# Score steps reordered over ticks, and three pieces of vector work spread, in a two-layer hybrid decoder kernel

## The reference

```
z    = x W_in                                   # 13 feature tiles, 4 value tiles, 10 gate tiles
o    = [GLA heads | retention heads | HGRN2 heads](z)      # gated linear recurrences
x    = LayerNorm(ALPHA x + o W_out)
q    = x W_q ; s1, s2 = q subkeys               # 8 heads, 2 x 128 keys
top 16 of s1, of s2, then of the 256 sums       # 16 experts a head, 128 a token
x    = LayerNorm(ALPHA x + sum_e gate_e gelu(u_e . x) v_e) # u_e, v_e: gathered rows of 1024
x    = x + (p W_ple) sigmoid(x W_gate)          # "embedding"
```

```
score[i, j] = sum_k q[i, k] k[j, k] exp(b[i, k] - b[j, k])   for j <= i,  b = running sum of log decay
```

## Time and profile before

| what | value |
|---|---|
| timed runs | 4085.25, 4070.53, 4074.74 us, median 4074.74 |
| profiled execution, own time | 4068.89 us |
| its span | 4067.1 us |
| granted TensorE clock, mean | 0.94 |
| busy: TensorE, VectorE, ScalarE, GpSimd | 3526.3, 2538.4, 1025.4, 2533.5 us |
| DMA read from HBM | 1259.74 MB, mean 312 GB/s with what was written |

### The profile page before, as it was taken

One profiled execution on the slowest core, in us unless ns is written; L12 is line 12 of the kernel. 1 busy time (PEld: TensorE's weight loads), 2 busy tenths in 40 slices (PEclk: granted clock), 3 DMA queues, 4 the chain that ended last, 5 costly groups with the idle time before them and its releaser, 6 DMA issues. The chain is left out here.

```text
span 4067.1 us, 42088 instructions
## 1 busy us (share of the span) xinstructions
PE 3526.3 (87%) x13480; PEld 2019.6 (50%) x13480; DVE 2538.4 (62%) x6604; ACT 1025.4 (25%) x2150; POOL 2533.5 (62%) x2420
## 2 busy tenths in 40 slices
PE   8787698999999799798999799999999877787878
PEld 6576364555555365344566256545555434222434
DVE  2535986766357985667557985567636798645442
ACT  2231132332122223222322222233312222211211
POOL 0212447877675655877765655687766666777773
PEclk9778799999999899999999999999999989999999
DMA  5015888888999898888999988888999989999996
GB/s 183 21 64 183 287 328 320 302 322 328 350 356 372 324 354 333 320 312 294 349 340 386 364 289 318 290 320 308 339 336 343 379 301 358 385 374 362 370 398 228
DMA packets 331050, 1270.02 MB, mean 312 GB/s; under 512 B 38336, under 2 KB 39616, under 8 KB 313808
## 3 DMA queue, kind: packets, MB, share of 16 engines
q0 software_dynamic: 299520, 1090.65, 73.0%
q1 hardware_dynamic: 31312, 176.67, 11.4%
HBM read 1259.74 MB, written 7.44 MB: 312 GB/s over the span
## 5 line engine op out<-in xcount | busy, mean ns | idle before, releaser
L819 PE MATMUL Y<-GV,DIAG 128*128 128x512 f32 x4096 | 1993.3, 624 | 315.4 <-DMA GV<-in_vtab,IDX 249.9
L1759 DVE SCALAR_TENSOR_TENSOR GU<-GU,X 128x1024 f32<-128x1024 f32 x1024 | 1241.4, 1230 | 511.2 <-DMA GU<-in_utab,IDX 508.9
L1038 POOL DMA_INDIRECT GU<-in_utab,IDX x1024 | 1152.5, 1125 | 641.4 <-DVE GU L1759 295.8
L1038 POOL DMA_INDIRECT GV<-in_vtab,IDX x1024 | 1146.1, 1119 | 597.8 <-PE Y L819 374.2
L819 PEld LDWEIGHTS Y<-GV,DIAG 128*128 128x128 f32 x4096 | 767.2, 197 | 1285.1 <-issue 985.9
L514 PE MATMUL A<-XT,WR 128*128 128x264 f32 (+1 forms) x2496 | 579.8, 388 | 18.1 <-ACT R L1252 10.5
L1285 ACT ACTIVATE DIAG<-C,WGT 128x128 f32<-128x128 f32 x1024 | 371.5, 392 | 749.1 <-PE Y L819 625.8
L514 PEld LDWEIGHTS A<-XT,WR 128*128 128x128 f32 x2496 | 481.3, 193 | 146.2 <-issue 74.9
L974 POOL TENSOR_TENSOR R<-R 128x256 f32<-128x256 f32 (+3 forms) x256 | 130.1, 541 | 164.6 <-DVE R L1437 88.9
L567 PE MATMUL SCP<-R,C 128*32 128x64 f32 (+3 forms) x512 | 104.6, 361 | 109.9 <-DVE R L1469 109.6
L733 PE MATMUL D<-WR,R 96*128 96x256 f32 (+3 forms) x800 | 189.9, 395 | 11.5 <-POOL R L992 11.5
(11 more groups left out here) (216 smaller groups left out, 2897.3 us busy)
## 6 DMA issues: line engine op xcount, KB each, us to landing
WR<-in_wstream SPq DMA_DIRECT2D x96, 1024.0 KB, 7.8
WR<-in_wstream SPq DMA_DIRECT2D x36, 1280.0 KB, 9.1
GU<-in_utab,IDX POOLq DMA_INDIRECT x1024, 6.5
GV<-in_vtab,IDX POOLq DMA_INDIRECT x1024, 6.5
R<-in_lnp SPq DMA_DIRECT2D x14, 512.0 KB, 7.1
SS<-in_st_in SPq DMA_DIRECT2D x12, 384.0 KB, 4.8
out_st_s<-SS SPq DMA_DIRECT2D x12, 384.0 KB, 6.2
WR<-in_wstream SPq DMA_DIRECT2D x16, 256.0 KB, 6.5
```

Of the source, the lines that this page charges most:

```text
L819: last = nc.tensor.matmul(Y[0:rows, c], scaled, GV[:, v % RV, c], start=(j == 0), stop=(j == end - 1))
L1038: pool.indirect_dma_start(ring[:, i % places, :], None, table, bass.IndirectOffsetOnAxis(ap=idx, axis=0)).then_inc(fetched[i % places], 16)
L1759: nc.vector.scalar_tensor_tensor(out=u, in0=u, scalar=1.0, in1=X[:, tile_of(g), :], op0=ALU.mult, op1=ALU.mult, accum_out=SCORE[:, g % 2, ...
```

## The change

A score step's VectorE work turns round and is split: products(k) come at "sc", low(k + 1) at the new key "lw" one tick later. ScalarE's pexp(k + 1) moves from "sp" to the new key "px", two ticks after "sc". GpSimd and TensorE keep "sp". In the first mixer, where all ticks are -1, only the order on VectorE changes. Block 1's searches take one and a half ticks a part (ticks 30 to 76). Block 7's begin at 58 ticks after the start of the fourth step, and take 54 ticks (834 to 886). The samples of layer 1 are searched in ticks 804 to 832. Embedding 2 is spread up to tick 868. Mixers, the other searches and the other embeddings keep their ticks.

```diff
-FOLLOW = {"z": [("zd", 1)], "rot": [("rotd", 1)], "sc": [("sp", 1)], ...
+FOLLOW = {"z": [("zd", 1)], "rot": [("rotd", 1)], "sc": [("sp", 1), ("lw", 1), ("px", 2)], ...
...
-        _spread(_own, STEP_AT[_s] + _lead, STEP_AT[_s] + (SPREAD if MIXED[_s] is not None else 70))
+        _spread(_own, STEP_AT[_s] + _lead, STEP_AT[_s] + (SPREAD if MIXED[_s] is not None else 98))
...
     if _s == 0:
-        _searches(1, [_a + i for i in range(PH * 4)])
+        _searches(1, [_a + i * 3 // 2 for i in range(PH * 4)])
     if _s + 1 < STEPS4:
...
+        if _s == 2:
+            _ticks[PH * 4:] = [STEP_AT[3] + 58 + i * 54 // (PH * 4) for i in range(PH * 4)]
...
-    _a = STEP_AT[2 * _L + 1] + SEARCHED + 2
+    _a = STEP_AT[2 * _L + 1] + (SEARCHED + 2 if _L == 0 else 28)
...
 ScalarE, at each of the four places of a score step:
-                        yield "sp", s, step
+                        yield "px", s, step
                         pexp(step + 1)
...
 VectorE:
                 def build_scores(step):
+                    products(step)
                     if step < 15:
+                        yield "lw", s, step
                         low(step + 1)
-                    products(step)
...
 and at each of its four places:
-                        build_scores(step)
+                        yield from build_scores(step)
```

More of the change, by code:

```diff
@@ L139 @@
           ("e", 4): 7}
-FOLLOW = {"z": [("zd", 1)], "rot": [("rotd", 1)], "sc": [("sp", 1)], "b": [("kt", 1), ("ky", 2), ("dl", 3)],
+FOLLOW = {"z": [("zd", 1)], "rot": [("rotd", 1)], "sc": [("sp", 1), ("lw", 1), ("px", 2)], "b": [("kt", 1), ("ky", 2), ("dl", 3)],
           "e": [("tn", 1), ("hn", 1), ("os", 2), ("td", 2)], "c": [("cg", 1)],
```

## The result

The changed kernel takes 4021.4 us (median of 4 runs, 4012.2 to 4026.7), the kernel before 4073.4 (4 runs, 4070.5 to 4085.3). The ratio is 0.9859, 95% interval 0.9840 to 0.9878: 57 us less, between 50 and 65. (The two medians differ by 52 us, which lies inside that interval; the ratio is what is used from here on.) The forecast was 4016 us.

The account below looks back on a forecast made before the run. No engine alone was taken as the bound: engines waiting in a chain first, then GpSimd, VectorE or DMA by stretch. Savings 15 + 26 + 8 + 10 = 59 us gave 4016 us as median, range 3972 to 4060.

Parts of the forecast that it names:

- late pieces: Ticks 800 to 886: levelling block 7's and layer 1's sample searches and embedding 2 uses idle DMA; 10 us, bounds 0 and 16.
- order, first mixer: Before the gathers: products no longer stand behind the minimum's wait for GpSimd; 15 us saved, bounds 0 and 25.
- order, three score stretches: Mixers beside the gathers: the minimum's wait leaves the path to the score sums; 26 us saved, bounds 0 and 53.
- block 1's spread: Ticks 30 to 76: a third of the searches moves to where VectorE has free time; 8 us saved, bounds -8 and 13.
- 7 to 11 us each: Expected sign: each of the three stretches with score steps beside the gathers shortens by this much.
- DMA share up by 0.02 to 0.03: Expected sign: DMA share rises this much in the three stretches with score steps beside the gathers.
- Rival A: Score stretches: VectorE running beside GpSimd's subtractions lengthens them, costing 41 us against 26 gained; 4042 us, worst 4057; chance 0.20.
- Rival B: Score steps: products wait for the later exponential, costing 71 us plus 12 in the first mixer; 4099 us at worst; chance 0.07.
- under 20 us of free VectorE time: Stretch 600 to 660 us: the 25 us of block 1's searches moved there must fit under this free time.
- rival C: Whole kernel: every removed wait lies on the path, so all 107 us come back; 3968 us; chance 0.13.

## Why the prediction came out, point by point

The last column is from the lengths of the term's own stretches, means of the traces with the piece against means of those without it (for the late pieces ticks 800 to 912: 325 against 343 us; for block 1 ticks 30 to 76).

| term | forecast | timed runs | its stretches |
|---|---|---|---|
| order, first mixer | 15 | 21 (15 to 27) | 18; first dot 16 to 20 earlier |
| order, three score stretches | 26 | 20 | 25 |
| block 1's spread | 8 | -6 (-13 to 1) | -4 to -6 |
| late pieces | 10, at most 16 | 21 (14 to 29) | 18 |
| sum | 59 | 56 of the parts; 57 (50 to 65) together | 55 to 57 |

*Order.* Right in mechanism and about right in size. Products stood behind the minimum's wait; out from behind it, TensorE's wait went from 110 to 45 us, further than the 60 forecast. VectorE's wait before the minimum fell only to 98.5, not under 90. The forecast gave half of the wait in the score stretches to the bound on GpSimd and DMA. For GpSimd the run with half of the subtractions bears this out: it shortened the same three stretches by 28.6 us more, though it can't tell GpSimd's occupied time from an earlier subtraction. GpSimd was busy or between two issues for 92% of these stretches before and 94% after, where the prediction had 94% before. "7 to 11 us each" came as 8.3, 6.7 and 9.2; "DMA share up by 0.02 to 0.03" as 0.00 to 0.02.

*Rival A*, GpSimd slowed by VectorE beside it, needed longer subtractions. They took 529 ns where they had taken 541, within what they vary without the new order. The port rule of the Trainium skill (SBUF — State Buffer, "SBUF: two separate sides"), by which a GpSimd instruction and a VectorE instruction with two SBUF inputs block each other, may hold for single instructions, as the earlier trace rows agree; in the sum it cost nothing here. The likely reason, not tested, is that VectorE does the same instructions as before and only stands elsewhere.

*Rival B*, the late exponential, was there but small: 14.6 us of new waits in the first mixer, where the products follow the minimum at once, paid out of a larger gain; beside the gathers it is 5.0 us, and the run with the tick at one shows no cost of the later tick.

*Block 1: this step failed.* The prediction put the moved work "under 20 us of free VectorE time". It read VectorE as the bound since VectorE waited for no gather there, and capped the gain by TensorE's 13.0 us. In the run of block 1 alone that wait still stands, so it had nothing to do with the searches that were moved:

```profile
PE D L501 <- DVE XT L1343: 13.0, 1, 13.0
```

TensorE was busy without a break in ticks 40 to 70, before and with the spread; relief of VectorE was passed on to waits for ScalarE and TensorE, and the later searches then held up the gathers in ticks 61 to 76. A gain of 8 us is excluded; a loss is seen in the searches' own stretch (4 to 6 us), while the timed runs alone don't tell it from nothing.

*Late pieces: mechanism right, size off.* The mis-sized term was the unused DMA capacity, 16 us, taken from the busy share (0.88 over both stretches, against 1.00 behind them). Bytes give another answer: 144 us at 310 GB/s are 44.6 MB, which take 114 us at the 393 GB/s behind it, so 30 us were free. Ticks 800 to 842 gained 29.8 (2.7 us a tick, where the forecast had about 3.0). That these two figures agree so closely is partly luck: the changed kernel moved only 42.7 MB there (115 us at 371 GB/s) and 51.1 MB in ticks 842 to 886, against 47.9 before. These 3 MB, moved one stretch later, take 8 us at 393 GB/s, and 8.7 us went back. So the bound by bytes is 30 and not 16, and some 18 to 21 of it were had. What keeps the rest isn't shown; dealing the searches more thinly didn't bring it.

The errors of the sum, 14 us too much for block 1 and 11 too little for the late pieces, nearly cancelled, as did the smaller ones of the two order terms. That is luck: the total was closer than its terms. One slip of the prediction: its rival C comes to 3968 us, and the range that is said to start from C starts at 3972.

## What to carry to other kernels

In an in-order queue put work whose inputs are there ahead of work that waits for another engine, above all where the latter is for the next step; that order was worth 35 us here without moving any tick. Before vector work is moved out of a crowded stretch, look at what else is full there and at what its engine will wait for next: moved to where the DMA was full the work cost little, while taking it away from beside a TensorE that was busy all the time gained nothing. Measure free DMA capacity in bytes a second against a full stretch of the same kernel, not in busy share.

## What the runs showed of the hardware that was not expected

The DMA engines count as 0.88 busy while they move 310 GB/s, and 1.00 busy at 393 GB/s, with the same kind of gather: a busy share of 0.88 stood for 0.79 of the throughput. The trace of the kernel before shows where the difference lies: the gathers' packets of 4096 bytes take 159 ns at the median in both stretches, but 186 ns in the mean where the share is 0.88, and 167 ns where it is 1.00. There 5.8% of them took over 300 ns, here 1.4%. Why single packets take so long isn't shown.

The granted clock of the first mixer's stretch rose from 0.73 to 0.78 for the same work, with fewer stalls. TensorE's busy time in it fell from 115.5 to 110.6 us. So some 5 of the 17 us gained there can be put down to its instructions taking less time, and 12 to less standing still; no run separates what the clock alone did.
